# The samples' paged attention, moved from a stage of its own into the stages ahead of it

## The reference, cut to what matters

```python
q, k, v, iq, ik, iw, rq, rk, rv, rg = even_project(h, w_in, pos)      # one token for each of 8 samples
ik_past = cik[page_table].reshape(b, past, D_IDX)                     # past = 8 pages of 128 keys
ik_all = jnp.concatenate([ik_past.astype(ik.dtype), ik], axis=1)
idx = indexer_topk(iq, iw, ik_all, pos, k_sel)                        # 256 of 1025 keys
kg = jnp.where(in_past, ck[page, off], k[bi, nidx])
vg = jnp.where(in_past, cv[page, off], v[bi, nidx])
att = sparse_attend(q, kg, vg, idx, pos, rel_bias)                    # 8 heads of 64: softmax(q k / 8 + bias) v
```

## Time and profile before

| | |
|---|---|
| median of 3 runs | 3991.7 us (3985.01 to 3997.84) |
| the profiled execution's own time | 3990.57 us |
| its span (first to last instruction) | 3989.0 us |
| PE busy | 3445.2 us, 86% |
| DVE busy | 1831.0 us, 46% |
| ACT busy | 1086.6 us, 27% |
| POOL busy | 1051.1 us, 26% |
| granted TensorE clock over the span | 0.911 |

### The profile page before, as it was taken

One profiled execution on the slowest core, in us unless ns is written; L12 is line 12 of the kernel. 1 busy time (PEld: TensorE's weight loads), 2 busy tenths in 40 slices (PEclk: granted clock), 3 DMA queues, 4 the chain that ended last, 5 costly groups with the idle time before them and its releaser, 6 DMA issues. The chain is left out here.

```text
span 3989.0 us, 57770 instructions
## 1 busy us (share of the span) xinstructions
PE 3445.2 (86%) x20584; PEld 3168.3 (79%) x20584; DVE 1831.0 (46%) x3075; ACT 1086.6 (27%) x1873; POOL 1051.1 (26%) x737
## 2 busy tenths in 40 slices
PE   6889968737469999999959988898875999999998
PEld 5439966621359999999948888888865999999998
DVE  3699938761322221212136777777772121212122
ACT  3412204400133221213122444333433231213132
POOL 2002203210213222221124444445443332221222
PEclk8859987858779999999969999999987999999999
DMA  3011230063321111111122222222214111111111
GB/s 115 21 27 47 80 106 1 1 239 99 113 78 47 48 47 48 42 47 48 64 40 73 78 81 86 69 81 64 71 65 152 56 48 48 42 48 47 47 47 65
DMA packets 338555, 261.94 MB, mean 66 GB/s; under 512 B 51646, under 2 KB 307662, under 8 KB 336694
## 3 DMA queue, kind: packets, MB, share of 16 engines
q1 hardware_dynamic: 317174, 208.61, 17.4%
q10 hardware_dynamic: 11520, 25.24, 2.0%
q0 software_dynamic: 9728, 26.47, 1.9%
HBM read 217.36 MB, written 44.74 MB: 66 GB/s over the span
## 5 line engine op out<-in xcount | busy, mean ns | idle before, releaser
L228 POOL TENSOR_TENSOR w_low_sb<-w_loaded_sb,w_high_sb 128x1024 fp32r<-128x1024 f32 (+1 forms) x230 | 555.2, 2414 | 1936.1 <-ACT w_high_sb L222 1924.6
L245 PE MATMUL psum<-act_high_sb,w_high_sb 128*128 128x344 f32 (+1 forms) x2544 | 816.1, 321 | 30.9 <-PEq L186 17.2
L245 PE MATMUL psum<-act_low_sb,w_high_sb 128*128 128x344 f32 (+1 forms) x2544 | 814.4, 320 | 0.0
L245 PE MATMUL psum<-act_high_sb,w_low_sb 128*128 128x344 f32 (+1 forms) x2544 | 814.2, 320 | 0.0
L245 PE MATMUL psum<-second_high_sb,w_high_sb 128*128 128x344 f32 x1704 | 545.5, 320 | 0.0
L245 PE MATMUL psum<-second_low_sb,w_high_sb 128*128 128x344 f32 x1704 | 544.3, 319 | 0.0
L245 PE MATMUL psum<-second_high_sb,w_low_sb 128*128 128x344 f32 x1704 | 544.2, 319 | 0.0
L245 PEld LDWEIGHTS psum<-act_high_sb,w_high_sb 128*128 128x128 f32 (+1 forms) x2544 | 478.3, 188 | 32.6 <-issue 32.3
L245 PEld LDWEIGHTS psum<-act_high_sb,w_low_sb 128*128 128x128 f32 (+1 forms) x2544 | 478.6, 188 | 0.4
L245 PEld LDWEIGHTS psum<-act_low_sb,w_high_sb 128*128 128x128 f32 (+1 forms) x2544 | 478.4, 188 | 0.4
L222 ACT CAST w_high_sb<-w_loaded_sb 128x1024 fp32r<-128x1024 f32 (+1 forms) x230 | 239.5, 1042 | 650.5 <-PE psum L245 601.4
(11 more groups left out here) (414 smaller groups left out, 4789.5 us busy)
## 6 DMA issues: line engine op xcount, KB each, us to landing
w_loaded_sb<-in_w_up SPq DMA_DIRECT2D x64, 512.0 KB, 4.0
w_loaded_sb<-in_w_down SPq DMA_DIRECT2D x64, 512.0 KB, 3.6
w_loaded_sb<-in_w_in_odd SPq DMA_DIRECT2D x48, 512.0 KB, 3.9
ecay_sum_spread_sb<-decay_sum_scratch SPq DMA_DIRECT2D x8, 2048.0 KB, 9.7
w_loaded_sb<-in_w_in_even SPq DMA_DIRECT2D x28, 512.0 KB, 3.8
v_pages_sb<-in_cache_v ACTq DMA_DIRECT2D x40, 256.0 KB, 4.3
x_scratch<-x_sb SPq DMA_DIRECT2D x2, 4128.0 KB, 13.9
x_sb<-x_scratch SPq DMA_DIRECT2D x2, 4128.0 KB, 14.9
```

What stands on the lines that cost most here:

```text
L228: self.nc.gpsimd.tensor_tensor(self.wl[:, par, :, 0:width], self.wf[:, par, :, 0:width], self.wh[:, par, :, 0:width].bitcast(F32), ALU.sub ...
L245: ins = nc.tensor.matmul(out, w[:, par, k, 0:width], a[:, k, cols], start=n == 0, stop=n == 3 * KT - 1)
```

## The change

The stage `attend_samples` is gone. A class `Samples` holds the same work, cut into pieces that three earlier stages call.

- In `project_and_choose`, beside units 7 to 22, key pages go through in 16 halves of 4 pages. SP loads a half into a ring of three (`load_keys`). POOL multiplies it with the query, which was spread over the partitions by a DMA from memory, and adds the upper 32 numbers of each head to the lower 32 (`multiply_keys`). DVE sums the remaining 32 (`sum_keys`) between its rounds of the choice. ACT stores the samples' queries to memory after unit 3 with four DMAs of 4-byte pieces (`store_q`).
- The choice works in place: `match_replace` overwrites the scores, and the mark becomes one `tensor_scalar` with `is_gt`. The second buffer is gone.
- In `keys_and_values` the three sample steps come first, and the softmax's small steps stand between the others (`probs_pe`, `probs_dve`, `probs_act`). ACT issues the loads of 28 value pages into the weight buffers and the unused upper halves of the activations, and then does the exponentials.
- In `attend`, PE takes about 2.1 value pages after each `weigh`, for n = 0 to 29 (`values_pe`). DVE keeps the diagonal columns (`values_dve`), and SP loads the other 36 value pages.
- The unit loops of SP, POOL and ACT are written out. PE's is still a loop.

```diff
--- before.py
+++ after.py
+def choose_in_place(dve, tally, S, m8, step):
+    if tally.count:
+        dve.wait_ge(tally.sem, tally.value())
+    tally.up(dve.max(m8, S) if step % 2 == 0 else dve.match_replace(S, m8, S, TAKEN))
+def mark_in_place(dve, tally, S):
+    dve.wait_ge(tally.sem, tally.value())
+    tally.up(dve.tensor_scalar(S, S, TAKEN, None, ALU.is_gt))
+class Samples:
+    HALF, HALVES, KRING, VRING, FIRST, STEPS = 4, 16, 3, 7, 7, 30
...
+    def load_pages(self, eng, cache, place, m, sem):
+        with eng.Fori(0, self.HALF) as j:
+            page = eng.value_load(self.B.pages[0:1, bass.ds(j + m * self.HALF, 1)], min_val=0, max_val=NPOOL - 1)
+            eng.dma_start(place[:, bass.ds(j, 1), :],
+                          self.B.i[cache][0][bass.ds(page, 1)].rearrange("o p h d -> p o (h d)")).then_inc(sem, 16)
+    def store_q(self, act, u):
+        act.wait_ge(self.B.s_tile_free, u * 3 + 9)
+        with self.B.nc.allow_non_contiguous_dma("the samples' queries, once"):
+            for t in range(4):
+                act.dma_start(self.q_scratch[:, t * P:(t + 1) * P].rearrange("b p -> p b"),
+                              self.B.qkv[:, t, SEQ:TOK]).then_inc(self.s_q, 16)
+    def load_keys(self, sp, m):
+        b = m // 2
+        if m == 0:
+            sp.wait_ge(self.s_q, 64)
+        if m % 2 == 0:
+            if b >= 2:
+                sp.wait_ge(self.s_mul, 2 * (b - 1))
+            sp.dma_start(self.qb[:, b % 2, :], self.q_scratch[b:b + 1, :].to_broadcast([P, 512])).then_inc(self.s_qb[b % 2], 16)
+        if m >= self.KRING:
+            sp.wait_ge(self.s_red, m - self.KRING + 1)
+        self.load_pages(sp, "cache_k", self.kp[:, m % self.KRING], m, self.s_key[m % self.KRING])
+    def multiply_keys(self, pool, m):
+        nc, b = self.B.nc, m // 2
+        pool.wait_ge(self.s_qb[b % 2], 16 * (b // 2 + 1))
+        pool.wait_ge(self.s_key[m % self.KRING], 16 * self.HALF * (m // self.KRING + 1))
+        k = self.kp[:, m % self.KRING]
+        nc.gpsimd.tensor_tensor(k, k, self.qb[:, b % 2, :].unsqueeze(1).to_broadcast([P, self.HALF, 512]),
+                                ALU.mult).then_inc(self.s_mul, 1)
+        pool.wait_ge(self.s_mul, m + 1)
+        d = k.rearrange("p j (h d) -> p (j h) d", d=DH)
+        nc.gpsimd.tensor_tensor(d[:, :, 0:32], d[:, :, 0:32], d[:, :, 32:64], ALU.add).then_inc(self.s_prod, 1)
+    def sum_keys(self, dve, m):
+        nc, b, j0 = self.B.nc, m // 2, m % 2 * self.HALF
+        dve.wait_ge(self.s_prod, m + 1)
+        nc.vector.tensor_reduce(self.logit[:, b, j0:j0 + self.HALF, :].rearrange("p g h -> p (g h)"),
+                                self.kp[:, m % self.KRING].rearrange("p j (h d) -> p (j h) d", d=DH)[:, :, 0:32],
+                                AX_X, ALU.add).then_inc(self.s_red, 1)
...
+    def probs_act(self, act):
+        act.wait_ge(self.s_sub, 2)
+        flat = self.logit[:].rearrange("p b g h -> p (b g h)")
+        self.B.nc.scalar.activation(flat, flat, ACT.Exp).then_inc(self.s_exp, 1)
+        self.B.nc.scalar.activation(self.pown[:], self.pown[:], ACT.Exp).then_inc(self.s_exp, 1)
...
+    def place(self, m):
+        B, r = self.B, m % self.VRING
+        if r < 3:
+            a = (B.wf[:], B.wh[:].bitcast(F32), B.wl[:].bitcast(F32))[r]
+            return a.rearrange("p a k m -> p (a k m)").rearrange("p (j c) -> p j c", c=512)
+        a = (B.hh, B.hl)[(r - 3) // 2][:, 4:8, :].bitcast(F32).rearrange("p k c -> p (k c)")
+        c0 = (r - 3) % 2 * self.HALF * 512
+        return a[:, c0:c0 + self.HALF * 512].rearrange("p (j c) -> p j c", c=512)
+    def load_values(self, eng, m):
+        if m >= self.VRING:
+            eng.wait_ge(self.s_taken, m - self.VRING + 1)
+        self.load_pages(eng, "cache_v", self.place(m), m, self.s_value[m % self.VRING])
+    def values_pe(self, pe, n):
+        B, nc = self.B, self.B.nc
+        if n < self.STEPS:
+            for p in range(n * NS * PAGES // self.STEPS, (n + 1) * NS * PAGES // self.STEPS):
+                b, j, m = p // PAGES, p % PAGES, p // self.HALF
+                if p % self.HALF == 0:
+                    pe.wait_ge(self.s_value[m % self.VRING], 16 * self.HALF * (m // self.VRING + 1))
+                if j == 0 and b >= 2:
+                    pe.wait_ge(self.s_kept, b - 1)
+                out = B.psum[0:HA, 1 + 2 * (b % 2), :]
+                ins = nc.tensor.matmul(out, self.logit[:, b, j, :], self.place(m)[:, p % self.HALF, :], start=j == 0, stop=False)
+                if p % self.HALF == self.HALF - 1:
+                    ins.then_inc(self.s_taken, 1)
+                if j == PAGES - 1:
+                    nc.tensor.matmul(out, self.pownd[:, b, :], B.qkv_s[:, 2, :], start=False, stop=True).then_inc(self.s_pvd, 1)
+        for b in range(NS):
+            if n == self.ready(b) + 2:
+                self.to_columns(pe, b)
...
+    def to_columns(self, pe, b):
+        B, nc = self.B, self.B.nc
+        pe.wait_ge(self.s_kept, b + 1)
+        for t in range(4):
+            ins = nc.tensor.matmul(B.psum[:, 5, b * 4 + t:b * 4 + t + 1], self.own_cols[:, b % 2, t * P:(t + 1) * P],
+                                   B.ones[0:HA, 0:1], start=True, stop=True)
+        ins.then_inc(self.s_col, 1)
+    def values_dve(self, dve, n):
+        B, nc = self.B, self.B.nc
+        for b in range(NS):
+            if n == self.ready(b) + 1:
+                dve.wait_ge(self.s_pvd, b + 1)
+                if b >= 2:
+                    dve.wait_ge(self.s_col, b - 1)
+                nc.vector.tensor_tensor(self.own_cols[:, b % 2, :].rearrange("h (g d) -> h g d", g=HA),
+                                        B.psum[0:HA, 1 + 2 * (b % 2), :].rearrange("h (g d) -> h g d", g=HA),
+                                        B.ident[0:HA, 0:HA].unsqueeze(2).to_broadcast([HA, HA, DH]), ALU.mult).then_inc(self.s_kept, 1)
...
         def _(sp):
-            for base, src in ((0, w_qkv), (12, w_r)):
-                with sp.Fori(0, 6) as j:
-                    for e in range(2):
-                        B.load_weights(sp, j * 2 + (U0 + base + e), par(e),
-                                       src[bass.ds(j * 2 + e, 1)].rearrange("o p k m -> p (o k) m"))
+            for u in range(UNITS):
+                B.load_weights(sp, U0 + u, par(u), w_qkv[u] if u < 12 else w_r[u - 12])
+                if 0 <= u - smp.FIRST < smp.HALVES:
+                    smp.load_keys(sp, u - smp.FIRST)
         @block.gpsimd
         def _(pool):
-            with pool.Fori(0, 12) as j:
-                for e in range(2):
-                    B.split_low(pool, j * 2 + (U0 + e), par(e))
+            for u in range(UNITS):
+                B.split_low(pool, U0 + u, par(u))
+                if 0 <= u - smp.FIRST < smp.HALVES:
+                    smp.multiply_keys(pool, u - smp.FIRST)
...
+            for u in range(UNITS):
+                if u + 1 < UNITS:
+                    B.split_high(act, U0 + u + 1, par(u + 1))
+                if u >= 14:
+                    act.wait_ge(s_spill[u % 2], 16 * ((u - 12) // 2))
+                for t in range(NT):
+                    B.await_tile(act, U0 + u, t)
+                    out = B.qkv[:, u, tcols(t)] if u < 12 else stage[:, u % 2, tcols(t)]
+                    nc.scalar.copy(out, B.tile(par(u), t)).then_inc(B.s_tile_free, 1)
+                if u == 3:
+                    smp.store_q(act, U0 + u)
+                if u >= 12:
+                    act.wait_ge(B.s_tile_free, (U0 + u) * 3 + 9)
+                    act.dma_start(B.r_scratch[u - 12], stage[:, u % 2, :]).then_inc(s_spill[u % 2], 16)
...
         @block.vector
         def _(dve):
...
+            chains = [B.scores_s[:, 0:KEYS_S]]
+            chains += [B.scores[:, score_offset(i):score_offset(i) + (i + 1) * P] for i in range(EARLY, LATE)]
+            place = lambda c: best[0:NS, c, :] if c == 0 else best[:, c, :]
+            m = 0
+            for r in range(ROUNDS):
+                for step in (2 * r, 2 * r + 1):
+                    for c, S in enumerate(chains):
+                        choose_in_place(dve, s_step[c], S, place(c), step)
+                while m < smp.HALVES and 16 * m + 12 * 11 <= 11 * r:
+                    smp.sum_keys(dve, m)
+                    m += 1
+            for c, S in enumerate(chains):
+                mark_in_place(dve, s_step[c], S)
+            for m in range(m, smp.HALVES):
+                smp.sum_keys(dve, m)
...
-    steps = [(0, NBLK)] + [(1, b) for b in range(NBLK + 1)] + [(2, b) for b in range(NBLK + 1)]
+    steps = [(part, NBLK) for part in range(3)] + [(part, b) for part in (1, 2) for b in range(NBLK)]
...
+                smp.probs_pe(pe, n)
...
+                dve.wait_ge(s_kept, n + 1)
+                smp.probs_dve(dve, n)
+        @block.scalar
+        def _(act):
+            for m in range(smp.VRING):
+                smp.load_values(act, m)
+            smp.probs_act(act)
     B.top = mark
-def attend(B):
+def attend(B, smp):
...
```

(18 more changed lines are left out.)

379 lines of the change are left out of this document (153 added, 226 removed).

## The result

The changed kernel takes 3866.3 us (median of 4 runs, 3863.51 to 3878.42) against 3993.7 us beside it (4 runs, 3985.01 to 3997.84): ratio 0.969, 95% interval 0.9662 to 0.9717. The profiled execution took 3863.74 us, its span is 3862.0 us, 127.0 less than the 3989.0 of before.

What follows compares the result with a forecast made beforehand. The prediction took the samples' stage as a chain of DVE then PE, the projection as PE-bound, keys and values as waiting for DMAs. 3990.6 - 184.2 + 45.6 + 13 + 3 = 3868.0 us, forecast range 3842 to 3885.

Steps and rivals of the forecast that it cites:

- The stage removed, -184.2: Samples' attention stage: removed from one boundary to the next, barrier included, -184.2 us; the retention stage behind stays as it is.
- Values on PE, +46: Prompt's first four attention blocks: page products join PE's own work, 129 us against 83.4; bounds +36 and +83.
- the clock stays low: Prompt's first four blocks: PE's clock at a mean of 0.85, +23 us, total 3891; chance 0.13.
- Keys and values, +13: Keys-and-values stage: ACT's 28 page issues delay the exponentials, +10.9 us, and shared DMA engines add 2; bounds +5 and +25.
- one sign that I had named: Keys and values: sample exponential about 40 us after the first page issue, DVE waiting for it before its last four row copies.
- Projection, +3: Projection stage: key pages on POOL and DVE fit, with two margins of zero at the ring of three, +3 us; bounds 0 and +37.
- the POOL-bound rival: Projection stage: POOL's product takes 8.79 us instead of 4.56, so POOL sets the pace, +37 us, total 3902; chance 0.09.
- `max` and `match_replace` beside POOL: Projection stage: DVE's choice operations did not slow POOL's `w_low`, 2.40 us in the earlier trace.
- The lock: Projection stage: by the skill's rule sums are free of POOL, but four new marks each wait, at most 18 us of DVE.
- Full lock of the choice: Projection stage: choice and POOL run one after the other, +130 us, exposed ring loads up to another +100; chance 0.03.
- The queries' store: Projection stage: four DMAs of 4-byte pieces issued on ACT could delay its next cast, costing up to 15 us.
- Late value pages: Prompt's first four blocks: pages arrive late and PE waits for values, about +27 us, total 3895; chance 0.05.

Runs made afterwards that it cites:

- e4: The changed kernel with 48 of the 64 value page products on PE left out, all loads kept: 3871.8 us.
- e6: The changed kernel with 48 of 64 value page products left out and 32 extra 128x512 matmuls on PE in keys and values: 3878.8 us.
- e1: The changed kernel with the 28 value page loads of keys and values issued by POOL in place of ACT: 3867.2 us.
- e3: The changed kernel with ACT loading only 12 value pages in keys and values, and SP the other 52 in attention: 3864.4 us.
- e13: The changed kernel with DVE's key sums one round earlier, ACT loading 4 value pages ahead of the exponentials, SP the other 60 in attention: 3857.1 us.
- e8: The changed kernel with each of DVE's key sums one round of the choice earlier: 3871.2 us, projection 286.1 us against 288.2.
- e12: The kernel before with only the choice in place and its new marks: 3989.1 us, ratio 0.9978 to 0.9998.
- e7: The changed kernel with the samples' queries turned to rows on PE and stored by one DMA after unit 5: 3866.2 us.

## Why the prediction was right, step by step

The time was predicted as 3868 and measured as 3866.3. The mechanism held. The closeness of the number is in part luck, as errors of several us inside two terms cancelled.

- **The stage removed, -184.2.** Right: -184.7. Between the last DVE operation of attention (874.57) and the retention load (875.53) stands only the barrier.
- **Values on PE, +46.** Attention as a whole grew by 44.8, but not as forecast. The 83.4 us that I called four blocks hold two heads of the fifth. At the end of the same work (741.51) the stretch took 134.1 us and not 129, so +50.7, and the rest of attention, which I had left as it is, took 134.0 us instead of 139.9, so -5.9. In terms of the sum: PE's own work was forecast as 119.8 us; an estimate from the rounded clocks of the two new windows (120.96 x 0.97 and 9.23 x 0.60) is 123. Of the 6 us of bubbles 3.9 appeared; DVE did wait for finished samples (26.8 us in 8 waits), but it had the time. The low clock was forecast as 3 us at the entry and cost about 7 (an estimate, the rest of 134.1): the entry took 16.5 us at 0.78, some 3 us, as forecast, and the two heads behind the last sample another 3.7 at 0.60. That the clock falls there was in no term. Why the later blocks gained 5.9 us no run shows.
- **The rival "the clock stays low"** didn't occur, but e4 and e6 show how near it was: with a quarter of the products it does, and takes back nearly all that they save. I had argued from the samples' own dense stretch; from 16 us into the blocks on the mixed ones hold 1.00 with 64 pages. Over the whole of them the clock is 0.97 with 64 pages and 0.96 with 32.
- **Keys and values, +13.** The sum was right to the tenth, the step behind it only half: "it issues 28 page loads before it may do the exponentials" is one of two chains that ended together. The other is DVE's: new steps of its own, which I had priced at nothing, between key stores that share the DMA engines with the pages, which I had priced at 2 us on top. It ran in parallel and was as long (e1). So one sign that I had named failed: DVE didn't wait for the exponential before its last rows. With ACT's issues out of the way the stage moves with the pages ahead of the exponentials: 55.5 us with 28 (e1), 50.6 with 12 (e3), 47.0 with 4 (e13). The last 4.4 us above the 42.6 of before no run took apart; DVE's 9.4 us of new steps are the candidate.
- **Projection, +3.** Measured +2.1, from the place that the sum had named, the ring of three ahead of the last unit. The forecast for half 15 was POOL's start at 528 and `w_low` at 537.7. They came at 525.0 and 536.4, or 527.8 and 539.2 if this stage had begun where it did before (2.75 later). Half 12 held its margin. The last addition took 4.13 us instead of 2.4, and the product 4.89 instead of 4.6. These 2.0 us of lock together are as large as PE's only stall in the stage, 1.9 (argued from the rows; e8 took the stall away by moving the whole half, not the lock). The product was 4.6 as forecast, so the POOL-bound rival fell.
- **`max` and `match_replace` beside POOL.** I had read that they don't slow `w_low` from the earlier trace rows, but there the choice was over: its last round ends at 512 and DVE's marks at 516. The 21 `w_low` of before that ran up to 512 settle it, 2.36 to 2.41 us each.
- **The lock.** By the Trainium skill ("SBUF — State Buffer", "Who interferes with whom") `tensor_scalar` can enter a mode in which it and POOL lock each other out, and `tensor_reduce` never contends on trn2. The trace agrees with both: one mark of four took 5.13 us where it takes 0.67 beside an idle POOL (e12) and 2.45 in e8, where POOL was subtracting; all 16 sums took 1.196 to 1.220 us, the last one beside POOL's subtraction too. Full lock of the choice (`max`, `match_replace`) did not occur: POOL's products beside them stayed at 4.6.
- **The queries' store** I priced at up to 15 us by its issue on ACT. The issues took 2.31 us and delayed one cast by 2.4. Its real cost lay in the DMA engines, and was hidden (e7).
- **Late value pages** didn't occur, not even with 60 of the 64 loaded in attention (e13).

What stays open: why the clock falls in some stretches in which PE is busy and not in others, why attention's later blocks took 143 to 151 us over runs with the same instructions, and why the stretch behind retention's first load moves by 20 us. The granted clock differs there, but no run isolated it.

## What to carry to other kernels

When two chains end together, an experiment on either one shows nothing; take both away before saying that a cause is refuted. And work that is put beside other work on PE can't be priced by its duration alone: look at the granted clock of the stretch with it, without it, and with half of it. Compare stage by stage where the unchanged rest moves more than the effect.

## What the runs showed of the hardware

- **Less work at a lower clock.** The four blocks with 64, 32, 16 and 0 page products (the last without the samples' own values and columns too): 124.2, 103.8, 121.1 and 77.8 us, at mean clock 0.97, 0.96, 0.73 and 0.70. With 16 pages PE was busy for 38.6 of 40 us at 0.50, so a busy PE by the trace doesn't mean the high clock.
- **Pieces of 4 bytes fill the DMA engines.** The store of 8 queries (4 DMAs, 16 KB, issued at 319.77) kept the engines mostly busy from 320 to 340, with a tail to 343. The DMA view of the changed kernel from 315 to 350 (share of 16 engines; then KB and us to landing):

```profile
q10 hardware_dynamic: 4160, 0.02, 62.4%
q1 hardware_dynamic: 1574, 1.50, 40.8%
...
w_loaded_sb<-in_w_in_even SPq DMA_DIRECT2D x1, 512.0 KB, 18.9
```

  By that share a packet of the queue lasts 0.624 x 35 x 16 / 4160 = 84 ns on its engine. This is the record's time for a packet: the two shares add up to 1.03, so packets overlap in the record, and 84 ns is an upper bound of what one costs. In e7 the same stretch had a share of 0.16, and the load landed in 3.7 us.
- **Short DVE instructions in a row hold up POOL together.** The three marks behind the first, 0.5 to 0.6 us each, lie inside POOL's addition (530.00 to 534.13) and take 1.48 us; the addition was 1.7 us longer than its usual 2.40.
